# A hybrid decoder step on one core: the last two head pairs of each group go through TensorE in step

## What is computed

```python
CB = jnp.einsum('bclgn,bcsgn->bclsg', Cm, Bm)
Wm = CB[..., None] * Lmat * dt[:, :, None]
y_diag = jnp.einsum('bclsgr,bcsgrp->bclgrp', Wm, x)             # within a chunk
chunk_states = jnp.einsum('bclgn,bclgr,bclgrp->bcgrpn', Bm, decay_end * dt, x)
h = d[..., None, None] * h + s                                  # the state carried on
y_off = jnp.einsum('bclgn,bcgrpn,bclgr->bclgrp', Cm, h_prev, jnp.exp(Acum))
y = y_diag + y_off
```

## Time and profile before

| | us |
|---|---|
| median of 3 runs | 2839.18 |
| lowest and highest of them | 2838.67 and 2839.24 |
| the profiled execution's own time | 2838.66 |
| its span in the trace | 2836.9 |
| TensorE busy in the span | 2805.6 |
| VectorE busy | 1781.1 |
| ScalarE busy | 1168.1 |
| GpSimd busy | 299.9 |

### The profile page before, as it was taken

The page is one execution under the profiler, slowest core; times in us unless marked ns, Lnnn a source line. Parts: engine busy times, 40 slices in busy tenths (PEclk is TensorE's granted clock), DMA queues, the critical chain, the costliest instruction groups (busy, mean ns, idle before and its releaser), DMA issues.

```text
span 2836.9 us, 53278 instructions
## 1 busy us (share of the span) xinstructions
PE 2805.6 (99%) x19312; PEld 2755.1 (97%) x19312; DVE 1781.1 (63%) x2250; ACT 1168.1 (41%) x1729; POOL 299.9 (11%) x456
## 2 busy tenths in 40 slices
PE   8999999999999999999999999999999999999998
PEld 7899999999999999999999999999999999999998
DVE  7788878887888645545455556555555555555564
ACT  5554453544544333333333335433333333333553
POOL 3222221212222100000000001000000000000100
PEclk9999999999999999999999999999999999999999
DMA  7787887787878665555555554555555555555463
GB/s 201 207 211 185 207 224 182 196 214 192 210 185 208 173 181 149 149 147 149 150 152 144 148 149 143 162 149 148 148 148 149 150 145 151 149 150 155 134 181 112
DMA packets 893378, 474.15 MB, mean 167 GB/s; under 512 B 154089, under 2 KB 886689, under 8 KB 892977
## 3 DMA queue, kind: packets, MB, share of 16 engines
q1 hardware_dynamic: 819097, 431.02, 56.3%
q10 hardware_dynamic: 73528, 39.39, 4.8%
q0 software_dynamic: 672, 2.66, 0.2%
HBM read 447.50 MB, written 25.47 MB: 167 GB/s over the span
## 4 chain that ended last, share of the span: by engine, by line
PE 96%; DVE 1%; ACT 1%; DMA 1%; SPq 0%; issue 0%; POOL 0%; ACTq 0%; DVEq 0%; POOLq 0%
PE ps L1713 30%; PE ps L1714 30%; PE ps L1715 30%; PE ps L2102 1%; PE ps L1861 1%; PE ps L1956 1%; PE ps L1862 1%; PE ps L1819 1%; PE ps L1871 0%; PE ps L2115 0%; PE ps L1973 0%; SPq L598 0%; PE ps L2072 0%; DMA wm<-acum_s 0%; PE ps L2086 0%
## 5 line engine op out<-in xcount | busy, mean ns | idle before, releaser
L1713 PE MATMUL ps<-n_hi,whi 128*128 128x320 f32 x4144 | 1286.1, 310 | 1.8 <-DVE wlo L1086 1.2
L1714 PE MATMUL ps<-n_lo,whi 128*128 128x320 f32 x4144 | 1281.2, 309 | 0.0
L1715 PE MATMUL ps<-n_hi,wlo 128*128 128x320 f32 x4144 | 1281.2, 309 | 0.0
L1086 DVE TENSOR_TENSOR wlo<-raw,whi 128x1024 fp32r<-128x1024 f32 x746 | 921.2, 1245 | 460.5 <-ACT whi L719 459.5
L719 ACT ACTIVATE whi<-raw 128x1024 fp32r<-128x1024 f32 x746 | 785.0, 1057 | 831.1 <-PE ps L1715 753.6
L1713 PEld LDWEIGHTS ps<-n_hi,whi 128*128 128x128 f32 x4144 | 778.6, 188 | 5.1 <-DVE wlo L1086 1.7
L1714 PEld LDWEIGHTS ps<-n_lo,whi 128*128 128x128 f32 x4144 | 778.6, 188 | 1.4
L1715 PEld LDWEIGHTS ps<-n_hi,wlo 128*128 128x128 f32 x4144 | 778.5, 188 | 0.0
L1713 PE MATMUL ps<-c_hi,whi 128*128 128x320 f32 x1728 | 535.5, 310 | 2.9 <-DVE c_lo L1400 2.4
L1715 PE MATMUL ps<-c_hi,wlo 128*128 128x320 f32 x1728 | 533.9, 309 | 0.0
L1714 PE MATMUL ps<-c_lo,whi 128*128 128x320 f32 x1728 | 533.9, 309 | 0.0
(11 more groups left out here) (299 smaller groups left out, 1792.0 us busy)
## 6 DMA issues: line engine op xcount, KB each, us to landing
raw<-in_w_in SPq DMA_DIRECT2D x322, 512.0 KB, 4.5
raw<-in_w_ffn_gate SPq DMA_DIRECT2D x88, 512.0 KB, 4.5
raw<-in_w_ffn_up SPq DMA_DIRECT2D x88, 512.0 KB, 5.0
raw<-in_w_ffn_down SPq DMA_DIRECT2D x88, 512.0 KB, 4.2
raw<-in_w_ssm_out SPq DMA_DIRECT2D x64, 512.0 KB, 6.1
hq<-in_state_ssm SPq DMA_DIRECT2D x512, 32.0 KB, 3.0
hs<-in_state_ssm ACTq DMA_DIRECT2D x32, 512.0 KB, 5.4
out_ssm_sample<-hs ACTq DMA_DIRECT2D x32, 512.0 KB, 3.4
```

Source lines behind the costliest of these rows:

```text
L1086: tt(wlo[slot][:], raw[slot][:], whi[slot][:].bitcast(F32), SUB).then_inc(lo_split, 1)
L1713: mm(out, w_h, x_h, start=first, stop=False)
L1714: mm(out, w_h, x_l, start=False, stop=False)
L1715: return mm(out, w_l, x_h, start=False, stop=last)
```

## The change

The step `pair` is cut into three functions: `in_chunk`, `off_chunk` and `carry_in`. Pairs 0 and 1 go through them as before. At step `pair 2` TensorE now takes both pairs 2 and 3: in-chunk of 2, in-chunk of 3, C and turn of 2, of 3, carry of 2, of 3. Step `pair 3` is empty on TensorE. The waits go with their parts; those for `w_ready` and `cbm_ready` stand at pair 0 alone. Operands, banks, sizes and the other engines' programs are the same.

```diff
+                    if j == 0:
+                        pe.wait_ge(w_ready, 5 * g + 5)
+                        pe.wait_ge(cbm_ready, g + 1)
+                    pairs = {0: (0,), 1: (1,), 2: (2, 3), 3: ()}[j]
+                    for q in pairs:
+                        in_chunk(g, q)
+                    for q in pairs:
+                        off_chunk(g, q)
+                    for q in pairs:
+                        carry_in(g, q)
```

More of the change, by code:

```diff
@@ L1947, in turn_tails, with in_chunk, off_chunk @@
                 last.then_inc(tail_turned, 1)
+            def in_chunk(g, j):
+                if j % 2:
+                    pe.wait_ge(hn_added, 8 * g + (1 if j == 1 else 3))
+                if j == 2:
+                    pe.wait_ge(z_ready, 4 * g + 3)
+                for c in range(3):
+                    rows = P if c < 2 else NS
+                    for i in range(2):
+                        h = 2 * j + i
+                        quad_i = 2 * c + h // 4 if c < 2 else 4
+                        m = h % 4 if c < 2 else h
+                        last = mm(ps[i * HD:(i + 1) * HD, YD_BANKS[j], token_rows(c)],
+                                  xdt[0:rows, c, h * HD:(h + 1) * HD], wm[0:rows, quad_i, m * rows:(m + 1) * rows],
+                                  start=True, stop=True)
+                last.then_inc(yd_done, 1)
+            def off_chunk(g, j):
+                pe.wait_ge(h1_kept, g + 1)
+                pe.wait_ge(yo_kept, 2 * g + j // 2 + 1)
+                if j == 1:
+                    pe.wait_ge(yg_ready, 4 * g + 1)
+                if j == 2:
+                    pe.wait_ge(z_ready, 4 * g + 4)
+                if j == 3:
+                    pe.wait_ge(yg_ready, 4 * g + 2)
+                bank = YOFF_BANKS[j]
+                mm(ps[:, bank, 0:P], h1t[:, j * P:(j + 1) * P], bc[:, 1, token_rows(1)], start=True, stop=True)
+                turn(ps[:, bank, 2 * P:3 * P], yo[:, j * P:(j + 1) * P], ident[:]).then_inc(yoff_done, 1)
             def carry_in(g, j):
+                pe.wait_ge(x_stacked, 2 * g + 2)
                 if j == 2:
```

## The result

The changed kernel takes **2842.4 us** (median of 22 executions, 2839.38 to 2844.33), the kernel before 2839.1 us beside it (22 executions, 2837.95 to 2839.85). The ratio is 1.0012 with a 95% interval of 1.0006 to 1.0017, which is 1.7 to 4.8 us more: within 0.2%, as forecast (2842.1, range 2837.0 to 2843.8).

A forecast was written before the change was run, and what follows sets the result against it. TensorE, busy for 99% of the span, was taken to bound the kernel. Seams save 0.2 us a group, but unit x 0's wait makes each end 0.36 longer: 2839.18 + 2.9 = 2842.1 us, range 2837.0 to 2843.8.

The forecast's parts named there:

- The wait of unit x 0: At each group's end, unit x 0 waits for VectorE's first addition for pair 2; the end gets 0.36 us longer.
- The new seam: From pair 2's 64-row part to pair 3's full-row in-chunk part on TensorE: 0.26 us, bounds 0.15 to 0.36.
- what the order saves: From z, the start of unit z 3's last matmul, to unit x 0: 3.645 instead of 3.84 us, if nothing waits.
- Carry to addition: At a group's end, VectorE's first addition starts 0.63 us after pair 2's carry on TensorE.
- No second wait follows: Behind pair 2, work shifted by 1.2 us stays covered at the next weight piece and at unit x 1.
- The clock: Second rival: TensorE's clock falls after the eight group-end seams, 27 us, giving 2869 us; chance 0.05.
- The sum: Eight group ends at 0.36 us each make 2.9 us more, 1.2 to 4.6 with the bounds.
- The first rival: At the group ends the wait does not bind, only seams count: 8 x 0.2 to 8 x 0.31 less; chance 0.18.

The follow-up runs named there:

- carry_early: Changed kernel with pair 2's carry directly behind both in-chunk products, ahead of both C products, pair 3's carry last: 2838.83 us, ratio 1.0000 to before.
- products_only: Changed kernel with only the in-chunk products in step, then C product, turn and carry pair by pair: 2838.62 us, ratio 0.9999 to before.
- late_carry: Changed kernel with only the carries together, in-chunk, C product and turn pair by pair: 2844.17 us, ratio 1.0016 to before.

## Why the prediction was right, and where its steps failed

**The wait of unit x 0: right.** The first carry starts 2.63 us after z (predicted 2.635), the addition lasts 0.69, the load follows its end by 0.14 (predicted 0.15), and the second matmul starts 0.24 after the first. TensorE waits for VectorE's addition at seven ends, as forecast; at the eighth only the time of the weight load speaks for it.

**The new seam and what the order saves: right.** From pair 2's 64-row load to pair 3's is 0.85 us (360.43 to 361.28); less the 0.59 of a full-row part that leaves 0.26, the middle value. The gain of 0.2 us exists: carry_early, where nothing waits, goes from z to unit x 0 in 3.65 us, close to the prediction's 3.645, though in another order.

**Carry to addition: the term that was mis-sized.** I took 0.63 us from the earlier trace rows, where the addition starts at 362.02 with an idle time of 0.31 put down to TensorE's carry. It measured 0.51 in the changed kernel (362.23 to 362.74), in products_only and in late_carry alike, and 0.55 in carry_early, where the carry stands behind a part of another shape. The row of VectorE's operation ahead of it, in the kernel before, tells why:

```profile
361.16 0.55 DVE L1380 SCALAR_TENSOR_TENSOR chunk<-xs,c_own,ps 128x320 f32<-128x320 f32 x1 [0.92 <-PE ps L2102]
```

It ended at 361.71, and the addition came 0.31 later; in groups 2 to 7 of before this step is 0.30 or 0.31. So before, VectorE came from its own preceding operation just too late to take the carry at once, though the carry is named as the releaser. VectorE's wait instruction that stands ahead of the addition (line 1383) bears this out, before and in the changed kernel:

```profile
L1383 DVEq EVENT_SEMAPHORE  x1: 21/21/21, 361.9 to 361.9; - x1
```

```profile
L1383 DVEq EVENT_SEMAPHORE  x1: 21/21/21, 361.6 to 361.6; - x1
```

It comes 0.2 us after line 1380's end in both (361.71 and 361.36), though the carry starts 0.5 us before that instruction in one kernel and 0.6 after it in the other. So it goes by VectorE's own operation. Where VectorE had been idle for over a microsecond, the 0.51 is the step itself. No run changed VectorE's operation alone. At the other pairs the step from line 1380 to the addition is 0.19 or 0.20; why it is longer at pair 2 stays open. Group 1, to which the prediction gave up to 0.23 more for the 0.86 in the earlier trace rows, pays no more: its step is 0.51 too.

With 0.51 in the place of 0.63 the loss is 0.25 us a pass (113.63 - 113.38) instead of 0.36: 8 x 0.25 = 2.0 us where the prediction has 2.9. Seven of the eight are in the table (six passes and group 7's 0.21). Group 0's lies in the opening: from z to unit x 0's second matmul it takes 4.28 us where it took 3.98, so 0.30.

**"No second wait follows": wrong at the last group.** I looked for it at unit x 1 and at the fourth weight piece, and in groups 1 to 7 there is none. After group 7 the work behind the pair is not under cover: ScalarE's chain to the square root waits for the store of pair 3's states, which lands later, and TensorE already waited for the end of that chain (the 7.59 us busy of 10 in the earlier trace rows, which I had read for the clock alone). Measured against the one trace of before, it costs up to 0.4 us. The prediction followed VectorE's delay to the next weight piece's use, with six microseconds of cover, and not to the loads that the split sets off.

**The clock: the rival was wrong in its place.** At the eight seams the granted clock stays at 1.00, so the cost of 27 us is out. "TensorE: Matmul & The Clock Gate" of the Trainium skill, section "A second HAM failure mode: psum-queue depth-cycling", describes a kernel in which short, frequent idle times between groups of matmuls make the clock swing. This trace, with a wait of 0.17 us and a load gap of 0.60 once per 113.6 us, shows no swing; whether more frequent ones would bring it no run here shows. The half-clock stretch that exists begins at the end of one wait of 2.5 us after the loop and costs 1.3 to 1.5 us in some executions. The prediction had taken the full clock at 950 to 960 in one trace as evidence that such a wait does not matter.

**The sum.** 2.0 for the seams, up to 0.4 for the last group and, if the mean clocks tell the executions apart (half of them pay 1.5, few of before do), an estimated 0.6 for the clock: 2.6 to 3.0, beside 3.3 measured (1.7 to 4.8). The forecast of 2.9 was near for a reason that was partly luck: a term 0.9 too large stood where two small ones were missing.

**The first rival** (nothing waits, gain alone) fell for the change as made; carry_early is the kernel in which it holds. Its 8 x 0.17 = 1.4 us doesn't show in its median, 2838.83 beside 2839.21; 0.71 of it went again on the way to the first output piece.

## What to carry to other kernels

Batching like steps to save seams moves the last of them later; before doing it, find who waits for the first result of the batch, and count from the moved instruction to that wait, step by step. Here 0.2 us of seams were bought with 1.2 us of delay against 0.85 of cover; issuing the one result that is waited for early kept the gain in the pass. Then follow the delayed engine's later work to the transfers that it sets off: here loads came a microsecond later and nearer to a store that another engine waits for. And a wait's releaser in a profile is the one that came last by its records: look at what the waiting engine itself did just ahead of it before taking the step as the price of the dependence.

## What the runs showed of the hardware

In two of five profiled executions of one kernel, a stretch of 3.4 us at half the clock began in the last 0.1 and 0.4 us of a TensorE wait of 2.5 us; in the three others, with waits of 2.4 to 2.8 us, the clock stayed full. The stretch cost 1.3 to 1.5 us. ScalarE stood idle for 4.68 us ahead of a copy that waits for a state store in the changed kernel's first profile, and 3.73 in before's; a table load of 1.28 us stands behind that copy. Between an addition on VectorE and the first weight load that waited for it lay 0.14 us where a register instruction of TensorE carried the wait, in three kernels, and VectorE started an addition 0.51 us after the start of the carry that it waited for.
